# Low parts of the split weights displaced by 48, 64, 0 and 16 bytes, and eight wide then eight narrow matmuls in every other chunk

## What is computed

```
h = rms_norm(x, ln_pre_g)
proj = einsum('bsd,de->bse', h, w_in)              # 2048 x 19456: rnn x and gate, q, k, v, z, two merge gates
y_rnn = einsum('bsc,cd->bsd', hr * silu(rnn_gate), w_rnn_out)
y_attn = einsum('bsc,cd->bsd', o * silu(attn_gate), w_attn_out)
y = einsum('bsd,de->bse', merged, w_o);  x = x + rms_norm(y, ln_post_g)
...
for l in range(2):                                  # the layers of the second block
    u = rmsnorm(x, g_pre[l]) @ w_in_2[l]
    (a_cq, a_ckv, a_kr, a_z, b_q, b_k, b_v, b_z, c_q, c_k, c_v, c_z, gates) = split(u)
    o_a, o_b, o_c = three attentions over 8 heads each
    y = sum(sigmoid(gates[n]) * ((o_n * silu(z_n)) @ w_branch[l][n]) for n in range(3))
    x = x + y @ w_out_2[l]
```

## Time and profile before

| what | value |
|---|---|
| median of two runs | 3157.36 us |
| span of the profiled execution (first to last instruction) | 3154.9 us |
| TensorE matmul busy | 3134.1 us, 99% of the span, 18230 matmuls |
| TensorE weight load busy | 2741.8 us, 87% |
| VectorE busy | 2130.5 us, 68% |
| ScalarE busy | 1733.0 us, 55% |
| DMA, share of 16 engines | 58.9% |
| mean granted TensorE clock | 0.998 of 2.4 GHz |

### The profile page before, as it was taken

How to read it: one execution, slowest core, us unless ns; L and a number is a source line. 1 busy time by engine, 2 the same in 40 slices (tenths; PEclk the granted TensorE clock), 3 DMA queues, 4 the chain that set the end, 5 groups by cost and what they waited for, 6 DMA issues and landing times.

```text
span 3154.9 us, 52176 instructions
## 1 busy us (share of the span) xinstructions
PE 3134.1 (99%) x18230; PEld 2741.8 (87%) x18230; DVE 2130.5 (68%) x2741; ACT 1733.0 (55%) x2291; POOL 0.2 (0%) x4
## 2 busy tenths in 40 slices
PE   9999999999999999999999999999999999999999
PEld 7888888888888788888888888888888888888888
DVE  7677575666667687766666555777776666655575
ACT  5685444444445556656555555645665656555563
POOL 0000000000000000000000000000000000000000
PEclk9999999999999999999999999999999999999999
DMA  7656655555556555565556655566556565665555
GB/s 230 194 168 200 198 187 166 183 177 172 181 167 208 178 168 163 156 198 173 174 171 192 184 181 182 181 198 186 158 157 202 170 179 167 192 189 180 178 185 175
DMA packets 569809, 571.67 MB, mean 181 GB/s; under 512 B 26352, under 2 KB 565488, under 8 KB 569712
## 3 DMA queue, kind: packets, MB, share of 16 engines
q1 hardware_dynamic: 569712, 570.42, 58.9%
HBM read 568.25 MB, written 2.10 MB: 181 GB/s over the span
## 4 chain that ended last, share of the span: by engine, by line
PE 97%; DVE 1%; ACT 1%; DMA 0%; SPq 0%; issue 0%; ACTq 0%; DVEq 0%
PE pg L537 91%; PE pa L771 1%; PE pa L788 1%; PE pa L537 1%; PE pa L778 1%; PE pa L747 1%; PE pa L789 1%; DVE hl L1276 0%; PE pa L704 0%; DMA raw<-w_o 0%; PE pa L878 0%; DMA raw<-w_in 0%; ACT hl L933 0%; SPq L456 0%; DVE uT L1357 0%
## 5 line engine op out<-in xcount | busy, mean ns | idle before, releaser
L537 PE MATMUL pg<-hT,hl 128*128 128x512 f32 x11456 | 2030.6, 337 | 1.1 <-DVE hl L1276 1.1
L537 PEld LDWEIGHTS pg<-hT,hl 128*128 128x128 f32 x11456 | 1750.9, 188 | 261.1 <-DVE hl L1276 4.2
L1276 DVE TENSOR_TENSOR hl<-raw,hl 128x1024 fp32r<-128x1024 f32 (+1 forms) x1071 | 1256.0, 1209 | 314.5 <-ACT hl L933 306.8
L933 ACT ACTIVATE hl<-raw 128x1024 fp32r<-128x1024 f32 (+1 forms) x1071 | 1084.0, 1044 | 313.1 <-PE pg L537 293.8
L537 PE MATMUL pg<-uT,hl 128*128 128x256 f32 (+1 forms) x3712 | 639.1, 333 | 15.9 <-DVE uT L1357 7.5
L537 PEld LDWEIGHTS pg<-uT,hl 128*128 128x128 f32 x3712 | 558.4, 190 | 92.2 <-issue 14.2
L941 ACT ACTIVATE corr<-pg 128x512 f32<-128x512 f32 x286 | 170.3, 596 | 843.0 <-PE pg L537 843.0
L537 PE MATMUL pg<-hl,hT 128*128 128x256 f32 (+1 forms) x1792 | 317.9, 336 | 0.0
L1283 DVE TENSOR_TENSOR work<-pg,corr 128x512 f32<-128x512 f32 (+1 forms) x154 | 105.8, 687 | 303.7 <-ACT corr L941 303.5
L537 PEld LDWEIGHTS pg<-hl,hT 128*128 128x128 f32 x1792 | 274.9, 188 | 40.7
L1283 DVE TENSOR_TENSOR gat<-pg,corr 128x512 f32 (+1 forms) x71 | 48.9, 689 | 139.4 <-ACT corr L941 139.4
(11 more groups left out here) (191 smaller groups left out, 1369.2 us busy)
## 6 DMA issues: line engine op xcount, KB each, us to landing
raw<-w_in SPq DMA_DIRECT2D x791, 512.0 KB, 4.7
raw<-w_br SPq DMA_DIRECT2D x96, 512.0 KB, 4.3
raw<-w_out SPq DMA_DIRECT2D x64, 512.0 KB, 4.7
raw<-w_rnn SPq DMA_DIRECT2D x32, 512.0 KB, 4.8
raw<-w_o SPq DMA_DIRECT2D x32, 512.0 KB, 5.0
raw<-w_att SPq DMA_DIRECT2D x16, 512.0 KB, 4.4
raw<-w_uq SPq DMA_DIRECT2D x16, 384.0 KB, 4.0
tab<-tabs SPq DMA_DIRECT2D x5, 896.0 KB, 7.2
```

What stands on the lines that cost most here:

```text
L537: return nc.tensor.matmul(out, lhsT, rhs, start=start, stop=stop, skip_group_check=True)
L933: nc.scalar.activation(hl4[:, j % 2, 0, a:a + n], raw[:, bass.ds(j % 2 * UC + a, n)], ACT.Copy)\
L1276: tt(hl4[:, j % 2, 1, a:a + n], raw[:, bass.ds(j % 2 * UC + a, n)], hl4[:, j % 2, 0, a:a + n].bitcast(F32), ALU.subtract).then_inc(lo_done, 1)
```

## The change

Two things are changed.

1. **The low parts are displaced.** `hl` grows from 8192 to 8272 columns (320 bytes more per partition). Slot 1 starts 48 columns (192 bytes) later than before. The low part of slot 0 moves by 12 columns (48 bytes) in its first half and 16 (64 bytes) in its second, that of slot 1 by 0 and 4 columns (0 and 16 bytes), each counted from its slot's start. `hT`, `uT` and all tensors behind them start 320 bytes later. The high parts stay on multiples of 64 bytes from the start of `hl`. All views of `hl` are now lists of slices from one function, `part`; the copies and subtractions write as many columns as before, and no instruction is added.
2. **The order in odd chunks.** In `unit`, for all forms but "t" and where `cj` is odd, `side` is replaced by `(APART,)`: all wides of a half, then all its narrows, in both halves, whatever `SIDE` said for it. Some 500 of about 1,050 halves run so. Even chunks keep their order.

```diff
-RUNS = -1
+RUNS, APART = -1, -2
...
+LO_SHIFT, LO_ROOM, SLOT = ((12, 16), (0, 4)), 40, 2 * UC + 48
...
-        hl = sb("hl", 4 * UC, F32R)
+        hl = sb("hl", 4 * UC + 2 * LO_ROOM, F32R)
...
-        hl4 = hl[:, :].rearrange("p (s h n) -> p s h n", s=2, h=2)
+        def part(j, e, h, a=0, n=UC // 2):
+
+            first = j % 2 * SLOT + e * UC + h * UC // 2 + (LO_SHIFT[j % 2][h] if e else 0) + a
+            return hl[:, first:first + n]
+
...
-                if RUNS in side and len(ks) == 4 and ks[0] % 8 == 0:
+                if APART in side or RUNS in side and len(ks) == 4 and ks[0] % 8 == 0:
                     for k in ks:
                         for s in range(subs):
                             wide(k, s)
...
             def unit(u, j, c, cj, op, first, last, form="f", subs=2, ready=None, halves=(0, 1), first_parts=None, side=()):
 
+                if form != "t" and cj % 2 and first_parts is None:
+                    side = (APART,)
...
-                    nc.scalar.activation(hl4[:, j % 2, 0, a:a + n], raw[:, bass.ds(j % 2 * UC + a, n)], ACT.Copy)\
+                    nc.scalar.activation(part(j, 0, h, 0, n), raw[:, bass.ds(j % 2 * UC + a, n)], ACT.Copy)\
...
-                    tt(hl4[:, j % 2, 1, a:a + n], raw[:, bass.ds(j % 2 * UC + a, n)],
-                       hl4[:, j % 2, 0, a:a + n].bitcast(F32), ALU.subtract).then_inc(lo_done, 1)
+                    tt(part(j, 1, h, 0, n), raw[:, bass.ds(j % 2 * UC + a, n)], part(j, 0, h, 0, n).bitcast(F32),
+                       ALU.subtract).then_inc(lo_done, 1)
```

More of the change, by code:

```diff
@@ L539, in split_view @@
             def split_view(j, n):
-                return [hl4[:, j % 2, h, :].rearrange("p (k n) -> p k n", n=n) if UC % n == 0 else
-                        hl4[:, j % 2, h, 0:UC // n * n].rearrange("p (k n) -> p k n", n=n) for h in range(2)]
+                return [[part(j, e, k * n // (UC // 2), k * n % (UC // 2), n) for k in range(UC // n)] for e in range(2)]
             def in_order(ks, subs, side, wide, narrow):
-                if RUNS in side and len(ks) == 4 and ks[0] % 8 == 0:
+                if APART in side or RUNS in side and len(ks) == 4 and ks[0] % 8 == 0:
                     for k in ks:
@@ L567, in feature_major @@
                     ks, subs, side,
[L568 to L569 removed]
+                    lambda k, s: mm(pg3[:, b + s, :], wh[k - base][:, s * P:s * P + P], op[:, k, :], start and k == ks[0], False),
+                    lambda k, s: mm(pg3[:, b + s, S:], wl[k - base][:, s * P:s * P + P], op[:, k, 0:S], False,
                                     stop and k == ks[-1]))
@@ L575, in token_major @@
                     ks, 2, side,
-                    lambda k, s: mm(pg3[:, b + s, :], op[:, k, s * P:s * P + P], both[:, k - base], start and k == ks[0], False),
-                    lambda k, s: mm(pg3[:, b + s, S:], op[:, k, S + s * P:S + s * P + P], hiw[:, k - base], False,
+                    lambda k, s: mm(pg3[:, b + s, :], op[:, k, s * P:s * P + P], both[k - base], start and k == ks[0], False),
+                    lambda k, s: mm(pg3[:, b + s, S:], op[:, k, S + s * P:S + s * P + P], hiw[k - base], False,
                                     stop and k == ks[-1]))
             def apart_view(j, n):
-                return [hl4[:, j % 2, h, :].rearrange("p (s n) -> p s n", s=2)[:, :, 0:n] for h in range(2)]
+                return [[part(j, e, h, 0, n) for h in range(2)] for e in range(2)]
             def both_view(j, n):
-                return hl4[:, j % 2, :, :].rearrange("p h (k n) -> p k h n", n=n)
+                views = []
+                for k in range(UC // n):
+                    h, a = k * n // (UC // 2), k * n % (UC // 2)
+                    apart = UC + LO_SHIFT[j % 2][h]
+                    first, a = j % 2 * SLOT, h * UC // 2 + a
+                    views.append(hl[:, first:first + 2 * apart].rearrange("p (e n) -> p e n", e=2)[:, :, a:a + n])
+                return views
             def opening(u0, c0, tiles_ready, first_parts, weights_parts=None, summed=None):
@@ L614, in unit @@
                 if form == "r":
-                    wh, wl = (w.rearrange("p h (k n) -> p h k n", n=P) for w in apart_view(j, 512))
+                    wh, wl = ([[w[h][:, k * P:k * P + P] for k in range(4)] for h in range(2)] for w in apart_view(j, 512))
                 for h in halves:
```

24 lines of the change are left out of this document (12 added, 12 removed).

## The result

| what | before | changed |
|---|---|---|
| median of two runs | 3157.36 us | 3180.25 us (3179.6 to 3180.9) |
| span of the profiled execution | 3154.9 us | 3179.0 us |

The ratio is 1.0073 with a 95% interval of 1.0044 to 1.0103. The changed kernel is slower by 23 us, 0.7%: inside the 2% and inside the range, but it is no "no change".

What follows compares the result with a forecast made beforehand. TensorE, 99% busy, was taken as the bound through its pace between matmuls. Span 3154.9 + 1.5 (order) + 0 + 0 (displacement) = 3156.4; medians lie 2.5 us higher, so about 3158 us, range 3075 to 3195.

Steps and rivals of the forecast that it cites:

- the terms at nothing for ScalarE, VectorE, the waits and the DMAs: Part copies, subtractions, DMAs and TensorE's waits: same work, VectorE idle 0.98 us per low part as cover, so 0 us.
- The reading of the price: On TensorE at full clock, each matmul costs 13.3 ns over its own columns, 226 us or 7% of the span.
- the case held likeliest: TensorE's pace stays the same: chance 0.52, its own range 3151 to 3166 us.
- the rival of a larger price: Displaced low loads on TensorE cost more than 13.3 ns a matmul: chance 0.17, somewhat under half beyond 2% slower.
- the term of displacement on TensorE: Displaced weight loads on TensorE: price the same wherever a load lies, 0 us, within bounds of -100 and +90 us.
- makes the loads clash more: Four distances may throw TensorE out of step between high and low loads: 3188 or 3248 us; larger price, chance 0.17.
- A sign named in advance: A TensorE pace that differs between slots or halves, which have different displacements, would show that addresses matter.
- The rival of the smaller price: Displacement takes part of the low loads' price away: 3108 us at half, 3058 at all; chance 0.26.
- a sign that it was wrong: Any order keeping TensorE below 346 ns a pair over tens of microseconds would prove the prediction wrong.
- the term of the order: Some 500 halves turned to eight and eight, +0.003 us each: +1.5 us, with 6 us either way behind fp32 matmuls.
- The three rows: Steady halves of 16 matmuls: 2.77 us alternating, 2.77 eight and eight, 2.78 in sets of two and two.
- the four wides of the earlier trace: Behind fp32 matmuls four wides took 0.95 us, 237 ns each and not 225: TensorE out of step for a while.

Runs made afterwards that it cites:

- e6: Kernel before, order unchanged, with high parts at 192 and low parts at 256 bytes off a multiple of 512 from the streamed tensors everywhere: 3124.11 us, ratio 0.9896.
- e3: Kernel before, order unchanged, with only the low parts displaced, by 16, 32, 48 and 64 bytes in the four slot halves: 3165.03 us.
- e4: Kernel before, order unchanged, with high and low parts displaced alike, by 16, 32, 48 and 64 bytes in the four slot halves: 3176.67 us.
- e8: Kernel before, order unchanged, with all high parts at 192 bytes and low parts at 208, 224, 240 and 272 in the four slot halves: 3172.6 us.
- e11: Kernel before, order unchanged, with high parts at 192 and low parts at 240 bytes everywhere: 3171.27 us.
- e2: Order of the change alone, every tile at its address in the kernel before: 3182.13 us, ratio 1.0080.
- e5: e2 with the first contraction tile of each even chunk doing both wides, then both narrows: 3164.54 us, ratio 1.0023 to the kernel before.
- e9: e6 with wides and narrows alternating everywhere outside the two openings, no sets of two and two: 3129.49 us, ratio 0.9914 to the kernel before.
- e10: e6 with the order of the change: 3146.54 us, ratio 0.9967 to the kernel before.

## Why the prediction was right or wrong

**Right.** TensorE is the bound and nothing feeds it later: its waits, the low and the high part's durations stand where they were put, so the terms at nothing for ScalarE, VectorE, the waits and the DMAs hold. The outcome lies within 2% and in the range. The reading of the price, 13.3 ns a matmul from the counts, was right (its 16,960 matmuls leave out 208 of L537's, 1%), and so was that it is the only large sum there: e6 moved it by a quarter.

**Luck.** The sum itself, 3158 us, missed by 22 us, and the case held likeliest, 3151 to 3166, didn't come. What came is the rival of a larger price, given 0.17, together with a price of the order, and the range holds it because it was drawn for both signs. The two terms that were wrong don't add: had 20.6 and 24.9 us stood one on top of the other, the kernel would be at 3203 us, above the range. Nothing in the prediction says that they wouldn't.

**Wrong: the term of displacement on TensorE, 0.** The step was "I take it as a price for each load wherever it lies". Alone the displacement costs +20.6 us. Its evidence was void: the cases that it compared (wides and narrows in a row, alternating, the roles swapped) all have every tile at distance 0, so they vary the order and hold the address. Equal prices there say nothing of another address. It also counted over the low loads only, while in e3 moved low parts alone leave the alternating halves at 2.773 us; it takes high parts off 0 as well (e4, e8), which the change does by moving `hT`. The rival "makes the loads clash more", at a third of its bound, gave 3188 and came nearest in size and sign, but in its mechanism it is only half right: TensorE isn't thrown out of step at each change between high and low load, it settles in other steady patterns, and one pair of distances can have several (e11). A sign named in advance did show it: a pace that differs between slots and halves. The rival of the smaller price was possible too: (192, 256), one of the change's own four pairs, gives -33 us when all halves have it, and keeps TensorE at 340 ns a pair over tens of microseconds, which the prediction named as a sign that it was wrong.

**Wrong: the term of the order, +1.5 us with 6 either way.** Alone it costs +24.9 us. The three rows have the right price for a half of each order in the neighbourhood in which it stood, and it was multiplied by 500 for halves with other neighbours. Two things were missing: eight and eight behind eight and eight (0.02 us more, about 7 us in sum), of which the trace before has no case inside plain chunks, and the alternating half behind eight and eight (0.045 us more, about 16 us), a half that the change doesn't touch. A hint was there: the four wides of the earlier trace rows at 237 ns each show that TensorE can run at another pace behind fp32 work. It was priced as 0.08 us once for each such place, a transient that ends, and not as a pattern that stays until something ends it. The other row isn't even a slow recovery: in the half at 941.83 us the 0.08 us stand in the first step alone, 313 ns from the first wide's start to the second's, right behind the last fp32 matmul, and the rest goes at the usual pace.

**Why the two don't add.** With the displacement in, the alternating halves behind eight and eight don't take the pattern of 353 ns: their mean of 2.821 us in e2 is 2.799 in the changed kernel. With the displacement alone it is 2.800, but from other lengths: most even chunks have 2.826, 2.749, 2.800 and 2.811 us there and 2.783, 2.801, 2.807 and 2.811 in the changed kernel. So eight and eight hands on another sequence here too, one that happens to cost nearly the same; why is not known. The 374 halves of eight and eight take 2.809 us. So 350 x 0.023 + 374 x 0.033 = 20 us, and the rest of the 24 is in the halves behind fp32 matmuls and the other orders.

**The rule on ports.** The Trainium skill, "TensorE: Matmul & The Clock Gate", section "Step-by-step: what each phase is for", has two independent read ports, so that a weight load takes no read bandwidth from the running matmul. The runs don't bear out what the prediction drew from it, that addresses can't matter: with the same instructions in the same order, the addresses of the weight tiles alone moved the price of a float32r matmul from 13.3 ns to 10.0 (e6) and to 16.7 (e11's slow chains). Whether the two reads meet at a port or somewhere else isn't shown. The gap of N / 2.4 + 2.5 ns that the prediction took from the same page's section "Back-to-back issue gap" is given there for an isolated matmul, without the loads; the least that these runs show, with a load for each matmul, is N / 2.4 + 10.0 ns.

**Open.** What load and stream meet at, if it is these two, and with which period in the address isn't known: the pairs tried fit no rule in 16 or 64 bytes. That the clash lies between load and stream, and not between load and the writes of ScalarE and VectorE to `hl`, is argued from patterns that repeat to the nanosecond while those writes come once in 2.7 us; no run took the writes away. Whether a distance exists below 10.0 ns wasn't found out, nor was the change's displacement tried with the set of `e5`.

## What to carry to other kernels

A steady row prices an instruction order in the neighbourhood in which it stands; before multiplying it, look for a row of each order behind each other order, and for how long TensorE keeps a pattern that it was handed. A test that never varied the address can't say that the address doesn't matter, so give each operand stream of a kernel that is at the pace of TensorE an offset of its own and measure a few pairs. Measure offsets and order together, since what one of them is worth changes with the other: the order of this change costs 25 us with the distances of before, 22 us with (192, 256) and 2 us with those of the change.

## What the runs showed of the hardware

- A float32r matmul with a weight load of its own costs, at a granted clock of 1.00 (2.4 GHz), its columns plus 10.0 to 16.9 ns in steady alternating halves, by where the weight tiles lie against the streamed ones and by what came before: 2.720 (e6), 2.773 (before), 2.800 (e9), 2.826 (e11) and 2.831 us (e2) for the same 16 matmuls.
- One and the same loop of matmuls has several steady patterns: at distance 0, 346.6 ns a pair or 353; at (192, 256), 340 or 350; at (192, 240), 346.6 or 353, and 340 in a few halves. A pattern can last until other matmuls come between, 112 us in e9 and 198 us in e11. One pair of matmuls in another order can bring the fast one back (e5).
- The lowest price seen is 10.0 ns, in halves that alternate. Halves of eight wides and eight narrows don't reach it at the same addresses (2.773 to 2.787 us, e10).
- The streamed operand's address matters too: with the low part moved by 16 to 64 bytes, the value projections, which stream both parts, take 2.83 to 2.86 us a half in place of 2.77 while the other alternating halves stay (e3, one run).
